# Gated recurrence of the second block as one block triangle of scores, ahead of the memory heads

## The chip, the cores and the metric

The kernel runs on one core of one Trainium2 chip. The metric is the device time of the whole kernel in microseconds (us); the times given are medians over runs. The engines are TensorE (PE, with its weight loads PEld), VectorE (DVE), ScalarE (ACT), GpSimd (POOL), and SyncE (SP), which issues the weight stream.

## What is computed

The reference is a network of two blocks over 256 tokens of width 1024, all in float32. The second block has two layers. Layer 0 mixes with a gated linear recurrence (4 heads, keys of 96, values of 192, chunks of 64 tokens) and, beside it, with 4 heads of attention over a memory of 256 rows. Its core is this:

```python
def _gla(q, k, v, log_a):
    ...
    q_c = chunks(q) * (K ** -0.5)
    k_c, v_c, g_c = chunks(k), chunks(v), chunks(log_a)
    b = jnp.cumsum(g_c, axis=3)
    b_last = b[:, :, :, -1:, :]
    q_t = q_c * jnp.exp(b)
    k_t = k_c * jnp.exp(-b)
    k_end = k_c * jnp.exp(b_last - b)
    attn = jnp.where(causal, jnp.einsum('nbhck,nbhsk->nbhcs', q_t, k_t), 0.0)
    o_intra = jnp.einsum('nbhcs,nbhsv->nbhcv', attn, v_c)

    def step(state, inp):
        qt, ke, vc, dec = inp
        o = jnp.einsum('bhck,bhkv->bhcv', qt, state)
        state = dec[..., None] * state + jnp.einsum('bhck,bhcv->bhkv', ke, vc)
        return state, o
    ...
# second_block, layer 0
o = _gla(q, k, v, log_a)
o = o * lax.rsqrt(jnp.mean(jnp.square(o), axis=-1, keepdims=True) + HEAD_NORM_EPS)
mix = jax.nn.silu(r) * (o * a_norm_g)
mo = _mem_attn(qm, mkv[:, :, 0], mkv[:, :, 1])
y = jnp.concatenate([mix, mo], axis=-1) @ w_out
x = _layer_norm(DN_ALPHA * x + y, ln_mix_g, ln_mix_b)
```

The first block (attention, a bidirectional recurrence, a convolution, an MLP), the second layer of the second block (dilated attention) and the lookup stages behind both layers are the same before and after.

## The kernel before

All weights stream as panels of 1 MB through four slots. SP loads a panel into RAW when VectorE has freed the slot (`lo_ready`); ScalarE makes the high part (`hi`, L441, fp32r), VectorE the remainder (`lo`, L889), and TensorE multiplies in three products for each tile (`three`, L1460 to L1462: high by high, high by low, low by high). `hi_to(n)` and `lo_to(n)` in the programs of ScalarE and VectorE advance these two splits up to panel n; every engine's program is written out by hand in order, so where such a call stands decides what waits behind it. A panel's result stands in one of four banks PS, and `mixing_panel(u)` of ScalarE copies it out; `evicted` waits for that copy.

Layer 0 of the second block has 11 input panels (u = 0 to 10): 0 to 3 give the queries and keys GQ, GK, 4 the memory queries QM, 5 to 7 the values GV, 8 to 10 the gate rows GR. `half` runs a panel as 48 matmuls of 256 columns; in mode "rr" these are two token tiles of 24. Then come 4 output panels (`wide`, 24 matmuls of 512 columns each), whose inputs are XH and XL, the high and low part of the mixed rows, and then one panel of memory keys and values (`mem_panel(3)`).

After panel 3 TensorE makes the gate projection (L1749). ScalarE and VectorE form from it the log gates, their scan B, the three decay factors, and at L1162 to L1164 KE (keys to the end of the chunk), KTD (keys times the inverse decay) and QTD (queries times the decay). TensorE meanwhile runs panels 4 and 5. The memory heads follow (`attention_pe`, `attention_act`, `attention_dve`): scores of heads 0 and 1 (L1524), panel 6, and for each head turn (four transposes of the probabilities, L1537), the scores of the head after next, a panel, and values (L1547). The softmax runs on VectorE (maximum L861, scaled maximum L862, reciprocal L868, scaling L870) and ScalarE (exponentials L419, copies L406 and L410), with one `lo` behind each head on VectorE.

Only then comes the recurrence: transposes of KE (L1773), scores within the four chunks (L1779), mask (L1181, L1183, with the constant "causal"), products of keys and values for three chunks (L1787), the state STA updated on VectorE (L1191, L1193), and for chunk 0 to 3 the outputs: scores times values (L1801) plus queries times state (L1803), each chunk behind the state and the copy GO of the one before. ScalarE copies each chunk (L677) and squares it (L681), after having formed the sigmoid of all gates at once (L671, L465, L466). VectorE multiplies the gates and the norm in (L1197, L1199, L1202). 11 warm matmuls (L1445), 12 transposes (L1812), the splits to XH (L686) and XL (L1245), 7 warm matmuls, and the output panels begin. GpSimd reloads the turned memory rows into MEMH and MEML (L1423) when `gon_ready` tells that the gated rows are done, as these two share storage with GV, GR and GO.

Of the kernel before, what the change touches and what calls it, by code (L numbers as in the profile page):

```python
# [6 lines left out]
F32 = mybir.dt.float32  # L7
# [4 lines left out]
ALU = mybir.AluOpType  # L12
# [3 lines left out]
P = 128  # L16
# [82 lines left out]
for _n, _w in (("ident", 128), ("iota", 128), ("zero", 128), ("blk", 128), ("ones", 128), ("rot", 128),  # L99
               ("cos", 256), ("sin", 256), ("gscan", 64), ("causal", 64)):  # L100
    CONST[_n] = (_c, _c + _w)
    _c += _w
# [28 lines left out]
def build(nc, stream, x_in, mem_in, const_in, par_in, lb_in, par2_in, wg2_in, mask_in, lev_in, rows_in, sk_in, out):  # L131
    ctx = ExitStack()
    with ctx:
# [115 lines left out]
        KER = at("ker", [P, TT, 4 * GLA_K])  # L249
        ATT = at("att", [P, 8, GLA_C])  # L250
        STA = at("sta", [P, 4, GLA_V])
# [69 lines left out]
        UC = [[M[0], M[1]], [PS[0], PS[1]]]  # L321
# [110 lines left out]
        def _(act):  # L432
# [165 lines left out]
            for l in range(DEPTH):  # L598
# [19 lines left out]
                def mixing_panel(u):  # L618
# [15 lines left out]
                if l == 0:  # L634
# [16 lines left out]
                    mixing_panel(5)  # L651
                else:
                    mixing_panel(0)

                p0 = 6 if l == 0 else 1
                attention_act(act, a, 16 + 4 * l, MEM_H, HEAD ** -0.5, lambda n: MIX2[64 * (n % 2):64 * (n % 2) + 64, 6 + n // 2, :],
                              lambda n: 64 * (n % 2), PM2, PT2,
                              panel=lambda n: mixing_panel(p0 + n))
                p1 = p0 + MEM_H + 1
# [4 lines left out]
                if l == 0:  # L664
                    mix_high(6, 8)
                    hi_to(s0 + N_MIX2[l] + 3)
                    act.wait_ge(sem("ket_done"), 1)
                    for tt in range(TT):
                        ins = act.activation(KER[:, tt, :], M[2 + tt][:, 0:384], ACT.Copy)
                    a.step(ins, sem("ker_ready"))  # L670
                    a.step(act.activation(flat(RG[:]), flat(GR[:]), ACT.Exp, scale=-1.0))  # L671
                    sigmoid(flat(RG[:]), sem("rsig_ready"))
                    for ch in range(4):
                        rows = slice(64 * (ch % 2), 64 * (ch % 2) + 64)
                        act.wait_ge(sem("oc_done"), ch + 1)
                        for j in range(2):
                            ins = act.activation(GO[rows, ch // 2, 384 * j:384 * j + 384], M[2 + j][rows, 0:384], ACT.Copy)  # L677
# [1458 lines left out]
```

## Time and profile before

| what | value |
| --- | --- |
| median of 3 runs | 2829.1 us (2828.31 to 2829.38) |
| the profiled execution | 2834.74 us |
| its span | 2832.8 us |
| mean granted TensorE clock | 0.985 |
| PE busy | 2751.9 us |
| DVE busy | 1703.8 us |
| ACT busy | 1373.9 us |
| DMA | 516.02 MB, mean 182 GB/s |

The profile is of one execution. Times inside it count from the first instruction. A granted clock of 1.00 is 2.4 GHz, of 0.50 is 1.2 GHz. A float32 matmul that is not split into high and low parts shows as two records, so "x4" is two such matmuls. A busy engine is not the same as an engine that holds up the end: the chain of waits follows from the last instruction back to whatever released each step.

### The profile page before, as it was taken

The page shows a single profiled execution, that of the slowest core. Times are in us where ns is not written, and L with a number is a line of the kernel's source. Part 1 is how long each engine was busy: PE and PEld are TensorE (multiplying, and loading weights), DVE is VectorE, ACT ScalarE, POOL GpSimd, SP SyncE. Part 2 cuts the span into 40 slices and gives each one's busy share as a digit, 9 for nine tenths or more (in the row PEclk, how much of TensorE's full clock was granted, in tenths as well). Part 3 has the DMA queues.
Part 4 walks back from the last instruction along what each step waited for, and adds up shares of the span by engine and source line. Part 5 has one row for each costly group of instructions (what it writes and reads, how often), then busy time and mean ns, then how long its engine had stood idle before and what let it go on. Part 6 is the DMA issues. An engine that isn't in the chain of part 4 may idle for free.

```text
span 2832.8 us, 45743 instructions
## 1 busy us (share of the span) xinstructions
PE 2751.9 (97%) x18622; PEld 2490.2 (88%) x18622; DVE 1703.8 (60%) x2676; ACT 1373.9 (49%) x1727; POOL 135.6 (5%) x68
## 2 busy tenths in 40 slices
PE   8989999899999999999999999998999999999997
PEld 8869889699786999999999888987999999999886
DVE  5637546465453699945554566557799654555665
ACT  4445443554344358844444444344568644444443
POOL 0000000000000430000000000000600000000000
PEclk9999999999997999999999999999999999999999
DMA  5315552145542435666656566423446756565672
GB/s 212 105 60 199 191 212 90 60 167 193 186 149 79 160 139 201 233 252 222 207 208 216 210 240 252 180 92 135 150 141 247 282 194 222 194 220 201 231 265 89
DMA packets 74411, 516.02 MB, mean 182 GB/s; under 512 B 8273, under 2 KB 8545, under 8 KB 18593
## 3 DMA queue, kind: packets, MB, share of 16 engines
q1 hardware_dynamic: 58576, 424.70, 42.1%
q0 software_dynamic: 10208, 43.45, 4.5%
q10 hardware_dynamic: 5488, 45.94, 3.9%
q8 instruction: 97, 1.59, 0.2%
q14 instruction: 42, 0.34, 0.0%
HBM read 474.22 MB, written 39.85 MB: 181 GB/s over the span
## 4 chain that ended last, share of the span: by engine, by line
PE 88%; DVE 9%; ACT 1%; issue 1%; DMA 1%; ACTq 0%; DVEq 0%
PE lin L1460 17%; PE lin L1461 17%; PE lin L1462 17%; PE m L1461 8%; PE m L1460 8%; PE m L1462 8%; PE m L1921 4%; PE lin L1633 2%; DVE lo L889 1%; PE m L1577 1%; PE m L1445 1%; PE m L1598 1%; PE m L1801 0%; PE m L1900 0%; PE m L1821 0%
## 5 line engine op out<-in xcount | busy, mean ns | idle before, releaser
L889 DVE TENSOR_TENSOR lo<-raw,hi 128x2048 fp32r<-128x2048 f32 x357 | 816.1, 2291 | 680.7 <-ACT hi L441 679.6
L441 ACT ACTIVATE hi<-raw 128x2048 fp32r<-128x2048 f32 x403 | 768.8, 1910 | 488.4 <-PE m L1462 346.8
L1460 PE MATMUL lin<-xh,hi 128*128 128x256 f32 x3376 | 975.6, 289 | 13.4 <-DVE lo L889 5.6
L1461 PE MATMUL lin<-xl,hi 128*128 128x256 f32 x3376 | 957.1, 284 | 0.0
L1462 PE MATMUL lin<-xh,lo 128*128 128x256 f32 x3376 | 956.8, 283 | 0.0
L1460 PEld LDWEIGHTS lin<-xh,hi 128*128 128x128 f32 x3376 | 647.2, 192 | 22.5 <-DVE lo L889 6.8
L1461 PEld LDWEIGHTS lin<-xl,hi 128*128 128x128 f32 x3376 | 648.0, 192 | 3.7 <-issue 1.0
L1462 PEld LDWEIGHTS lin<-xh,lo 128*128 128x128 f32 x3376 | 647.4, 192 | 0.0
L1461 PE MATMUL m<-lo,ah 128*128 128x512 f32 x1024 | 402.9, 393 | 0.0
L1460 PE MATMUL m<-hi,ah 128*128 128x512 f32 x1024 | 400.7, 391 | 0.0
L1462 PE MATMUL m<-hi,al 128*128 128x512 f32 x1024 | 399.0, 390 | 0.0
L754 ACT ACTIVATE h<-lin 128x512 f32<-128x512 f32 x128 | 76.2, 596 | 353.6 <-PE lin L1462 330.2
L1460 PEld LDWEIGHTS m<-hi,ah 128*128 128x128 f32 x1024 | 192.4, 188 | 42.3 <-DVE al L1353 0.7
L1462 PEld LDWEIGHTS m<-hi,al 128*128 128x128 f32 x1024 | 192.3, 188 | 41.8
L1461 PEld LDWEIGHTS m<-lo,ah 128*128 128x128 f32 x1024 | 192.4, 188 | 37.3
L1921 PE MATMUL m<-ob,oa 128*128 128x128 f32 x1024 | 135.2, 275 | 0.0
L1921 PEld LDWEIGHTS m<-ob,oa 128*128 128x128 f32 x1024 | 125.3, 191 | 0.5
L1430 POOL TENSOR_TENSOR lo<-raw,hi 128x2048 fp32r<-128x2048 f32 x22 | 101.4, 4608 | 336.4 <-DVE lo L889 288.0
L1460 PE MATMUL lin<-hi,xh 128*128 128x256 f32 (+2 forms) x336 | 111.7, 332 | 3.8 <-DVE xl L904 2.3
L1461 PE MATMUL lin<-lo,xh 128*128 128x256 f32 (+2 forms) x336 | 109.6, 326 | 0.0
L1462 PE MATMUL lin<-hi,xl 128*128 128x256 f32 (+2 forms) x336 | 109.4, 326 | 0.0
L1337 DVE TENSOR_SCALAR ob<-cst,pb,pf 128x128 f32<-128x128 f32 x384 | 109.4, 342 | 0.0
(332 smaller groups left out, 2856.4 us busy)
## 6 DMA issues: line engine op xcount, KB each, us to landing
raw<-stream SPq DMA_DIRECT2D x403, 1024.0 KB, 4.8
gate_table<-stg ACTq DMA_DIRECT2D x16, 2048.0 KB, 10.7
g<-gate_table POOLq DMA_DIRECT2D x32, 1024.0 KB, 8.3
rows<-rows ACTq DMA_DIRECT2D x4, 1024.0 KB, 7.5
memh<-mem_turned_scratch POOLq DMA_DIRECT2D x3, 1024.0 KB, 5.5
meml<-mem_turned_scratch POOLq DMA_DIRECT2D x3, 1024.0 KB, 9.4
x_scratch<-x ACTq DMA_DIRECT2D x2, 1024.0 KB, 4.3
x<-x_scratch ACTq DMA_DIRECT2D x2, 1024.0 KB, 7.2
```

The source lines that it names most:

```text
L441: act.activation(HI[i % SLOTS][:], RAW[:, i % SLOTS, :], ACT.Copy).then_inc(hi_ready, 1)
L754: act.activation(H[:, s % AHEAD, :], PS[s % 4][:], ACT.Gelu).then_inc(sem("ge_ready"), 1)
L889: dve.tensor_tensor(LO[i % SLOTS][:], RAW[:, i % SLOTS, :], HI[i % SLOTS][:].bitcast(F32), ALU.subtract).then_inc(lo_ready, 1)
L1337: ins = dve.tensor_scalar(ob[:, j, :], cst("iota"), PB[:, 1, t + j:t + j + 1], PF[:, t + j:t + j + 1], ALU.is_equal, ALU.mult)
L1430: pool.tensor_tensor(LO[i % SLOTS][:], RAW[:, i % SLOTS, :], HI[i % SLOTS][:].bitcast(F32), ALU.subtract).then_inc(lo_ready, 1)
L1445: pe.matmul(bank[:, 0:256], cst("ident"), CST[:, 0:256], start=True, stop=True)
L1460: pe.matmul(out_, ah, bh, start=first, stop=False, **kw)
L1461: pe.matmul(out_, ah, bl, start=False, stop=False, **kw)
L1462: return pe.matmul(out_, al, bh, start=False, stop=last, **kw)
L1577: last[j] = pe.matmul(to[:, 64 * tt:64 * tt + 64].rearrange("p (b m) -> p b m", m=m), KS[o, d, t], halves(QS[o, d, t], m)[:, :, 1 - d, :], ...
L1633: pe.matmul(PS[1][:, 256 * ct:256 * ct + 256], DG[:, n % DIAGS, :], UP[:, ct, i:i + TOK], start=(i == 0), stop=(i == CONV_K - 1))\
L1921: ins = pe.matmul(M[k % 4][:, KEYS * t:KEYS * t + KEYS], oa[:, t, :], ob[:, t, :], start=True, stop=True)
```

## The change

The chunk states go. For each head the scores of all four chunks of queries against all chunks of keys at or before them are formed at once, as a block triangle: within a chunk from KTD and QTD, against the chunk before from KE and QTD, and against earlier ones from KE and queries that VectorE has multiplied by the decays of the chunks between (QA, QB, from the columns BL). AT0 holds the scores of the first 128 keys against 256 queries, AT1 those of the last 128 keys against the last 128 queries. The diagonal blocks of 128 are masked by GM, a full 128x128 causal mask that VectorE forms from "iota" and a column of P2 in place of the constant "causal"; the part of AT0 without mask is copied by ScalarE. The outputs are then 12 matmuls of 192 columns with AT0 and AT1 as weights.

The order: scores stand behind panel 6, panel 7 after them, then the value products, and the memory heads move into panels 8, 9 and 10. `half` calls `between(0)` between its two token tiles in mode "rr", and the memory heads' scores, turns and values stand there and between the panels. ScalarE and VectorE have this order written out instead of calling `attention_act` and `attention_dve`. On ScalarE each gate panel also goes through an exponential into RG when it is evicted, and `gate(j)` forms the sigmoid of that panel; the squares are 8 of 128 rows. VectorE multiplies each gate panel (`gated_rows`), and multiplies norm and gate into GO2 by head and token tile in 8 instructions, each pair of which raises `gon_ready`. The transposes begin at its second raise, the XH and XL splits go by pairs, the memory part is split between pairs 2 and 3, and the output panels wait for the first four rows of XH and XL, the last two for all. Warm matmuls are 9 and 4 in place of 11 and 7. GpSimd's reload waits for the fourth `gon_ready`.

The core of the diff:

```diff
+                        if u >= 8:
+                            ins = act.activation(RG[:, :, 256 * j:256 * j + 256], b[:].rearrange("p (t n) -> p t n", t=2), ACT.Exp, scale=-1.0)
...
+                    mixing_panel(6)
+                    for j in range(2):
+                        act.wait_ge(sem("gmask_ready"), j + 2)
+                        a.mark(act.activation(AT0[:, 2 * j:2 * j + 2, P:TOK], M[j][:].rearrange("p (h q) -> p h q", h=2)[:, :, P:TOK], ACT.Copy), sem("gcross_ready"))
+                    mixing_panel(7)
+                    for j, bank in enumerate((3, 0, 1, 2)):
+                        tt, c = j // 2, 2 * GLA_V * (j % 2)
+                        act.wait_ge(sem("gval_done"), j + 1)
+                        a.mark(act.activation(GO[:, tt, c:c + 2 * GLA_V], M[bank][:, 0:2 * GLA_V], ACT.Copy), sem("go_ready"))
...
+                    squares(0)
+                    exps(0)
+                    squares(1)
+                    exps(1)
+                    rstd(SMALL[:, 48:56], SMALL[:, 48:56], GLA_V, EPS, sem("grs_ready"))
+                    mixing_panel(8)
+                    turned(0)
+                    exps(2)
+                    gate(0)
+                    head_out(0)
+                    turned(1)
+                    exps(3)
+                    mixing_panel(9)
+                    head_out(1)
+                    gate(1)
+                    turned(2)
+                    mixing_panel(10)
+                    gate(2)
+                    head_out(2)
+                    turned(3)
+                    head_out(3)
...
+                    v.mark(later(QA[k96, :, 0:GLA_C], QTD[k96, :, 2 * GLA_C:3 * GLA_C], 1))
+                    v.step(later(QB[k96], QTD[k96, :, 3 * GLA_C:4 * GLA_C], 2))
+                    v.step(later(QA[k96, :, GLA_C:2 * GLA_C], QB[k96], 1), sem("glater_ready"))
+                    lo_to(s0 + 9)
...
+                        v.step(dve.scalar_tensor_tensor(out=out_, in0=cm, scalar=3.0e38, in1=bank.rearrange("p (h q) -> p h q", h=heads)[:, :, 0:P],
+                                                        op0=ALU.mult, op1=ALU.min))
+                        v.mark(dve.scalar_tensor_tensor(out=out_, in0=cm, scalar=-3.0e38, in1=out_, op0=ALU.mult, op1=ALU.max), sem("gmask_ready"))
+                    masked(AT1[:], M[2][:], 4, 1)
+                    masked(AT0[:, 0:2, 0:P], M[0][:], 2, 2)
+                    masked(AT0[:, 2:4, 0:P], M[1][:], 2, 3)
...
+                    head_max(0)
+                    head_max(1)
+                    lo_to(s0 + 10)
+                    head_scale(0)
+                    head_max(2)
+                    lo_to(s0 + 11)
+                    head_scale(1)
+                    head_max(3)
+                    gated_rows(0)
+                    head_scale(2)
+                    lo_to(s0 + N_MIX2[l] + 1)
+                    gated_rows(1)
+                    head_scale(3)
+                    gated_rows(2)
+                    dve.wait_ge(sem("dve_step"), v.count["dve_step"])
+                    dve.wait_ge(sem("grs_ready"), 1)
+                    dve.wait_ge(sem("go_ready"), 4)
+                    for h in range(4):
+                        c = slice(GLA_V * h, GLA_V * h + GLA_V)
+                        for tt in range(TT):
+                            ins = dve.scalar_tensor_tensor(out=GO2[:, tt, c], in0=GO[:, tt, c], scalar=SMALL[:, 48 + 4 * tt + h:49 + 4 * tt + h], in1=RG[:, tt, c],
+                                                           op0=ALU.mult, op1=ALU.mult)
+                        v.mark(ins, sem("gon_ready"))
...
+                    pe.wait_ge(sem("gqk_ready"), 1)
+                    def chunk(n):
+                        return slice(GLA_C * n, GLA_C * n + GLA_C)
+                    keys = slice(0, 64), slice(64, 128)
+                    def two_chunks(to, h, n):
+                        pe.matmul(to[keys[0], 0:GLA_C], KTD[k96, h, chunk(n)], QTD[k96, h, chunk(n)], start=True, stop=True)
+                        pe.matmul(to[keys[1], 0:P], KTD[k96, h, chunk(n + 1)], QTD[k96, h, GLA_C * n:GLA_C * n + P], start=True, stop=True)
+                        return pe.matmul(to[keys[0], GLA_C:P], KE[k96, h, chunk(n)], QTD[k96, h, chunk(n + 1)], start=True, stop=True)
+                    for h in range(4):
+                        ins = two_chunks(M[2][:, P * h:P * h + P], h, 2)
+                    ins.then_inc(sem("gsc_done"), 1)
+                    for j in range(2):
+                        for h in (2 * j, 2 * j + 1):
+                            to = M[j][:, 256 * (h % 2):256 * (h % 2) + 256]
+                            two_chunks(to, h, 0)
+                            pe.matmul(to[keys[1], P:P + GLA_C], KE[k96, h, chunk(1)], QTD[k96, h, chunk(2)], start=True, stop=True)
+                            pe.wait_ge(sem("glater_ready"), 1)
+                            pe.matmul(to[keys[0], P:TOK], KE[k96, h, chunk(0)], QA[k96, h, :], start=True, stop=True)
+                            ins = pe.matmul(to[keys[1], P + GLA_C:TOK], KE[k96, h, chunk(1)], QB[k96, h, :], start=True, stop=True)
+                        ins.then_inc(sem("gsc_done"), 1)
+                    mixing_panel(7)
+                    for u in (5, 6, 7):
+                        evicted(pe, s0 + u)
+                    def head_values(bank, tt, h0):
+                        for h in (h0, h0 + 1):
+                            to, c = M[bank][:, GLA_V * (h - h0):GLA_V * (h - h0) + GLA_V], slice(GLA_V * h, GLA_V * h + GLA_V)
+                            ins = pe.matmul(to, AT0[:, h, P * tt:P * tt + P], GV[:, 0, c], start=True, stop=(tt == 0))
+                            if tt == 1:
+                                ins = pe.matmul(to, AT1[:, h, :], GV[:, 1, c], start=False, stop=True)
+                        ins.then_inc(sem("gval_done"), 1)
+                    pe.wait_ge(sem("gmask_ready"), 2)
+                    head_values(3, 0, 0)
+                    pe.wait_ge(sem("gmask_ready"), 3)
+                    pe.wait_ge(sem("gcross_ready"), 2)
+                    head_values(0, 0, 2)
+                    head_values(1, 1, 0)
+                    head_values(2, 1, 2)
...
+                    evicted(pe, s0 + 4)
+                    def first_scores(c):
+                        if c == 0:
+                            pe.wait_ge(sem("go_ready"), 2)
+                            scores(0)
+                            pe.wait_ge(sem("go_ready"), 3)
+                            scores(1)
+                    def second(c):
+                        if c == 0:
+                            values(0)
+                            turn(1)
+                            scores(3)
+                    def third(c):
+                        if c == 0:
+                            turn(2)
+                    mixing_panel(8, first_scores)
+                    pe.wait_ge(sem("go_ready"), 4)
+                    turn(0)
+                    scores(2)
+                    mixing_panel(9, second)
+                    values(1)
+                    mixing_panel(10, third)
+                    values(2)
+                    turn(3)
+                    warm(9, PS[(s0 + N_MIX2[l]) % 4])
+                    values(3)
+                    for kt in range(6):
+                        if kt % 2 == 0:
+                            pe.wait_ge(sem("gon_ready"), (2, 3, 4)[kt // 2])
+                        if kt == 4:
+                            pe.wait_ge(sem("pt_ready"), 16 + MEM_H)
+                        for tt in range(TT):
+                            c = 256 * (kt % 2) + P * tt
+                            ins = pe.transpose(M[kt // 2][:, c:c + P], GO2[:, tt, P * kt:P * kt + P], cst("ident"))
+                        if kt % 2 == 1:
+                            ins.then_inc(sem("got_done"), 1)
...
+                        if u == 0:
+                            warm(4, PS[(s0 + N_MIX2[l] + 3) % 4])
+                        pe.wait_ge(sem("mix2l_ready"), u // 2 + 1)
```

Removed are the transposes of KE, KER, ATT, STA, the key and value products L1787, the per chunk outputs L1801 and L1803, the whole-array gate and norm products, and the wait of the recurrence for all panels and all memory heads.

## Rows read from the trace of the kernel before

**Rows 1.** The page, parts 1 and 4: busy time, and the chain by engine.

```profile
PE 2751.9 (97%) x18622; PEld 2490.2 (88%) x18622; DVE 1703.8 (60%) x2676; ACT 1373.9 (49%) x1727; POOL 135.6 (5%) x68
...
PE 88%; DVE 9%; ACT 1%; issue 1%; DMA 1%; ACTq 0%; DVEq 0%
```

**Rows 2.** Windows: busy us of PE, PEld, DVE, ACT, POOL; granted clock; DMA.

```profile
840.00:860.00 20.00, 19.56 (x149) 17.46 (x147) 5.34 (x5) 8.63 (x14) 0.00 (x0) 1.00 0.29 106
860.00:911.00 51.00, 46.27 (x181) 27.75 (x182) 18.28 (x27) 21.16 (x55) 1.06 (x2) 0.63 0.16 62
```

**Rows 3.** Chain of waits, recurrence and output panel: start, us, engine, tile, line.

```profile
860.03 0.88 PE m L1773 x8
...
895.96 7.21 PE m L1445 x22
...
908.08 0.50 PE lin L1460
```

**Rows 4.** Timeline of TensorE, 813 to 828: start, us, line, shapes, idle before.

```profile
813.96 1.14 PE L1524 MATMUL m<-kvl,qm 64*128 64x256 f32 x8
815.03 0.39 PE L1460 MATMUL lin<-hi,xh 128*128 128x256 f32 x1
...
820.77 0.28 PE L1462 MATMUL lin<-hi,xl 128*128 128x256 f32 x1
824.55 0.66 PE L1537 MATMUL m<-cst,pm 128*128 128x128 f32 x4 [3.50 <-DVE pm L870]
...
826.90 0.58 PE L1460 MATMUL lin<-hi,xh 128*128 128x256 f32 x1
```

**Rows 5.** Timeline of TensorE, 858 to 909.

```profile
860.84 1.15 PE L1779 MATMUL m<-qtd,ktd 96*64 96x64 f32 x32
...
904.32 3.19 PE L1445 MATMUL m<-cst 128*128 128x256 f32 x14
```

**Rows 6.** Timeline of VectorE, 815 to 909.

```profile
818.18 1.21 DVE L1164 SCALAR_TENSOR_TENSOR qtd<-gq,exa 96x1024 f32<-96x1024 f32 x1
819.43 2.29 DVE L889 TENSOR_TENSOR lo<-raw,hi 128x2048 fp32r<-128x2048 f32 x1
821.64 0.69 DVE L861 TENSOR_REDUCE small<-m 128x2 f32<-128x512 f32 x1
...
823.88 0.61 DVE L870 TENSOR_SCALAR pm<-pm,small 128x256 f32<-128x256 f32 x2
...
862.04 0.69 DVE L1181 SCALAR_TENSOR_TENSOR att<-cst,m 128x512 f32<-128x512 f32 x1 [0.67 <-PE m L1779]
...
878.38 1.39 DVE L1193 SCALAR_TENSOR_TENSOR sta<-sta,bl,lin 96x192 f32<-96x192 f32 x4 [10.75 <-PE m L1803]
...
905.46 2.44 DVE L1245 SCALAR_TENSOR_TENSOR xl<-m,p,xh 128x256 fp32r<-128x256 f32 x6 [1.94 <-ACT xh L686]
```

**Rows 7.** Timeline of ScalarE, 858 to 865.

```profile
858.59 0.60 ACT L626 ACTIVATE gr<-lin 128x512 f32<-128x512 f32 x1 [3.36 <-PE lin L1462]
...
861.85 1.48 ACT L671 ACTIVATE rg<-gr 128x1536 f32<-128x1536 f32 x1
```

**Rows 8.** Chain of waits between panels 7 and 8.

```profile
835.26 1.01 PE m L1547 x4
...
837.91 0.32 PE lin L1460
```

**Rows 9.** Windows at and after falls of the clock.

```profile
159.80:163.20 3.40, 1.93 (x9) 1.38 (x10) 1.42 (x6) 0.67 (x2) 0.00 (x0) 1.00 0.01 2
163.30:166.60 3.30, 3.30 (x9) 1.40 (x8) 1.44 (x5) 1.02 (x4) 0.00 (x0) 0.50 0.00 0
...
825.00:827.00 2.00, 2.00 (x7) 1.06 (x5) 1.52 (x1) 2.00 (x7) 0.00 (x0) 0.61 0.51 213
832.00:836.00 4.00, 4.00 (x30) 3.52 (x29) 0.00 (x0) 0.60 (x1) 0.00 (x0) 0.97 0.84 281
```

**Rows 10.** Timeline of GpSimd: the reload of the turned memory rows.

```profile
901.49 0.53 POOL L1423 DMA_DIRECT2D memh<-mem_turned_scratch  x1 [341.86 <-DVE go L1202]
```

More of the change, by code:

```diff
@@ L1165, in _, with later @@
                                                     op0=ALU.mult, op1=ALU.mult), sem("gqk_ready"))
-                p0 = s0 + (6 if l == 0 else 1)
-                lo_to(p0 + 3)
-                attention_dve(dve, v, 16 + 4 * l, MEM_H, HEAD ** -0.5, PM2, between=lambda n: lo_to(p0 + 4 + n))
+                    def later(out_, in_, ch):
+                        decay = BL[k96].rearrange("p (h n) -> p h n", n=4)[:, :, ch].unsqueeze(2).to_broadcast([GLA_K, 4, GLA_C])
+                        return dve.tensor_tensor(out_, in_, decay, ALU.mult)
@@ L1481, in half @@
                     for tt in range(TT):
+                        if tt == 1:
+                            between(0)
                         for k in range(KT):
@@ L1738, in _, with mixing_panel @@
                         half(HP_SHARED + u, "cc" if u < 3 else "rr", inst=6 if u == 0 else None)
-                def mixing_panel(u):
-                    half(s0 + u, "rr" if l == 0 and u >= 5 else "cc", inst=4 if l == 0 and u == 0 else None)
+                def mixing_panel(u, between=lambda c: None):
+                    half(s0 + u, "rr" if l == 0 and u >= 5 else "cc", inst=4 if l == 0 and u == 0 else None, between=between)
                 if l == 0:
@@ new lines, in _, with scores @@
+                    pe.wait_ge(sem("gmask_ready"), 2)
[5 more added lines that the diff above has]
+                    head_values(2, 1, 2)
+                    def scores(n):
+                        if n >= 2:
+                            pe.wait_ge(sem("exp_ready"), 16 + n - 1)
+                        o = slice(64 * (n % 2), 64 * (n % 2) + 64)
+                        for qt in range(2):
+                            ins = pe.matmul(M[n % 2][:, 256 * qt:256 * qt + 256], QM[o, n // 2, P * qt:P * qt + P], KVL[o, 256 * (n // 2):256 * (n // 2) + 256],
+                                            start=True, stop=True)
+                        ins.then_inc(sem("sc_done"), 1)
@@ new lines, in turn @@
+                    def turn(n):
+                        pe.wait_ge(sem("sm_ready"), 16 + n + 1)
+                        if n >= 1:
+                            pe.wait_ge(sem("pt_ready"), 16 + n)
+                        for kt in range(2):
+                            for qt in range(2):
+                                ins = pe.transpose(M[2][:, 256 * kt + P * qt:256 * kt + P * qt + P], PM2[:, n % 2, qt, P * kt:P * kt + P], cst("ident"))
+                        ins.then_inc(sem("pt_done"), 1)
@@ new lines, in values @@
+                    def values(n):
+                        pe.wait_ge(sem("pt_ready"), 16 + n + 1)
+                        if n >= 1:
+                            pe.wait_ge(sem("o_ready"), 16 + n)
+                        o = 64 * (n % 2)
+                        for kt in range(2):
+                            c = 512 + 256 * kt + 64 * n
+                            ins = pe.matmul(M[3][o:o + 64, 0:256], KVL[:, c:c + 64], PT2[:, n % 2, kt, :], start=(kt == 0), stop=(kt == 1))
+                        ins.then_inc(sem("pv_done"), 1)
```

208 lines of the change are left out of this document (87 added, 121 removed).

## Prediction

> **What bounds the kernel now.** I read the page first: TensorE is busy 97% of the span and carries 88% of the chain that ended last [rows 1]. What pays is therefore time taken off TensorE's own program, or time in which it waits or runs at the lower of its two clock levels. Then the windows: between the input panels it is at full level, and around the recurrence it averages 0.63 over 51 us [rows 2]. The chain of waits shows why: between the last input panel and the first output panel every link is the recurrence, with products L1773 and L1779, chunk states L1787, outputs L1801 and L1803 chunk after chunk behind the state update on VectorE, 22 records of warm matmuls, transposes, and the split into XH and XL [rows 3]. TensorE's timeline gives the ends of the stretch that I sum: panel 5 ends when the scores of heads 0 and 1 begin at 813.96, and the chain has the first output panel at 908.08 [rows 3, 4]. That is 94.1 us from 813.9. Everything behind 908.08 is moved as a whole.
>
> **What is removed.** From 860.03 to 908.08 lie 48.05 us that hold only the recurrence, its gates and the split [rows 3]. No weight panel runs there, and the clock was at 1.2 GHz for most of it: the 22 records of warm matmuls took 7.21 us [rows 2, 3]. The wait of 3.50 us for the first head's softmax goes too [rows 4], in its old form.
>
> **What stands in its place, in TensorE's order.** The work is 5 panels (6 to 10) and small pieces. I start at 813.9.
> - Panel 6: 48 matmuls, first start 815.03, last start 820.77 [rows 4], so 5.76 us with the last step; end 819.65. VectorE's qtd ends at 818.18 + 1.21 = 819.4 [rows 6]; the new wait for it costs about nothing. The mask tile GM is formed on VectorE ahead of the gate projection, in a wait of VectorE; nothing late depends on it.
> - Score stage: 4 heads of 256 columns, then 4 of 512, 3072 columns in 64-column tiles. L1779 did 1024 such columns (32 records, 16 matmuls) in 1.15 us [rows 5], with the two halves of the array alternating as here. So 3.4 us. Bounds: 2.7 us if the halves overlap fully, 5.5 us if not at all (3072 columns at 1.78 ns: 14 records, 7 matmuls of 256 columns on the full array, took 3.19 us [rows 5]). I take 3.4, the same tile form. QA, QB and QA again are 256 elements each on VectorE, at 0.41 as in L1245 [rows 6], ready at 820.7 while TensorE is still in the first four heads.
> - Panel 7: 5.76. Then TensorE waits for its eviction (0.60 on ScalarE [rows 7]): 0.7. This is a new wait; queued behind it are the value products and panel 8. The masks are long done: behind the weight split at 820.7 (2.29) VectorE needs 1.4 for the first and 0.8 for each of the others (0.69 for 512 elements [rows 6]), 826.1 in all, against panel 7's end at 828.8.
> - Value products: 12 matmuls of 192 columns on the full array, 0.34 us each by the same 1.78 ns, 0.38 by the two accumulating ones of 256 columns in 1.01 [rows 5, 8]: 4.2 us. They replace 28 matmuls of the same 192 columns on quarter and three-quarter tiles.
> - Panel 8 with scores 0 and 1 in its middle: 5.76 + 1.16 [rows 4]. It ends at 840.4.
> - A wait for the first softmax. From the scores at 836.3: matmuls 1.1, maximum 0.69 + 0.2 with its scaling, the second maximum 0.9, the weight split 2.29 that stands ahead of head_scale, then 0.17 + 0.61 and steps [rows 6]: 842.4. So 2.0 us idle, where the kernel before had 3.5.
> - turn(0) and scores(2): 1.65; panel 9: 5.76; in its middle values(0), turn(1), scores(3): 2.65, the distance from 835.26 to 837.91 [rows 8], and 0.2 of waiting, as one more split stands ahead of head_scale(1); values(1) 1.0; panel 10: 5.76, with turn(2) 0.6 in it. It ends at 860.2.
> - The tail. On TensorE: values(2), turn(3), 9 warm matmuls of 0.46 [rows 5], values(3), half of the transposes: about 7.4. Longer is the gate: evict 0.6, exponential 0.5, logarithm and exponential 0.63 each (512 elements; the whole array took 1.48 for 1536 [rows 7]), product 0.69, 8 products of 192 elements at 0.35 (L1193: 1.39 for 4), weight split 2.29, four XL pieces at 0.41 [rows 6]: 10.1. First output panel at 870.3.
>
> Sum: 5 x 5.76 = 28.8; 3.4 + 0.7 + 4.2 + 1.16 + 2.0 + 1.65 + 2.65 + 0.2 + 1.0 + 0.6 = 17.6; tail 10.1; together 56.5 against 94.1. Gain 37.6 us at full clock.
>
> **The clock.** In the kernel before, 3.5 us of idleness ahead of 824.55 put TensorE at the lower level, 1.2 GHz, just behind it [rows 9]. It cost: panel 7 took 835.26 - 826.90 = 8.36 instead of 5.76, and the turn and scores ahead of it 826.90 - 824.55 = 2.35 instead of 837.91 - 836.27 = 1.64 (836.27 is where values end): 3.3 us [rows 4, 8]. In the first block a stretch with 1.93 us busy of 3.40, all in small pieces, was at full level, and the one behind it at 0.50 [rows 9]. The new wait of 2.0 us lies between two small pieces, so I expect one fall there. It costs what one fall costs, 3.3, and nothing hides it, because from there to panel 10's end TensorE sets the pace and the tail hangs on panel 10. Net gain 34.3.
>
> **What else moves.** ScalarE gets an exponential more for each gate panel and 8 squares of 128 rows for 16 of 64 rows; up to panel 10 they lie beside panels, and hide as long as turned(n) is done before values(n): 846.1 against 846.9 for head 0. That 0.8 us is the thinnest cover; if it goes, TensorE waits by the excess. Splits of panels 9 and 10 on VectorE start 14 us later than before, so SP issues weights 13 and 14 later, at 841.5 and 847.2; with some 5 us to land they are there before ScalarE asks at 857.7 and later. On GpSimd the reload of the turned memory hangs on gon_ready, at 901.49 before [rows 10], now near 866, still 26 us ahead of its panel. The stage from the first output panel on has the same program; its own waits (the keys of the next product among them) may meet the clock differently, by which I allow half of one fall, 1.7 us, either way. The weight split of panel 12 now stands between the normed rows and XL: it is in the tail above.
>
> **A rule weighed.** In the trace a change of tile form costs a longer first matmul: 0.39 behind the scores at 815.03, where the later ones show 0.28 [rows 4]. The Trainium skill (TensorEngine Tiling (Array Packing), Key Properties) says that changing the tiling mode drains TensorE, while different tiles of one mode run in parallel. By the first half each inserted piece costs its own drain, which the distances above already hold; by the second half the score stage would come to its lower bound of 2.7, and the gain to 0.7 more.
>
> **Rivals.**
> - *No fall of the clock.* The clock stays at 2.4 GHz through the 2.0 us of waiting. For it: with 19.56 of 20 us busy from 840 to 860 the short waits between panels left it there [rows 2]; the one fall in this stretch had 3.5 us. Gain 37.6: 2791.5 us.
> - *Two falls or thin cover.* The score stage of 3.4 us, all on 64-column tiles, brings a fall of its own (3.3), or its halves do not overlap (+2.1), or values(0) waits. For it: the clock was down for most of the stretch of 64-row and 64-column tiles from 860 on [rows 2, 3]. Against: the scores at 813.96, on 64 rows, did no harm [rows 4]. 2829.1 - 34.3 + 3.3 = 2798.1, with the missing overlap 2800.2.
> - *Slower than before.* TensorE falls to 1.2 GHz in the score stage and does not come back until the four output panels are through. Then the 45 us of its work in the stretch (37.7 up to panel 10's end, 7.4 behind it) takes twice as long, which eats the gain and 2 us more, and the output panels (4 of as many columns as an input panel, so 23 us) take twice as long as well: 2829.1 + 2 + 23 = 2854. It decides from 75 us of TensorE's work at the lower level on. Against it: after the fall near 825 a single panel was enough for the clock to return: 0.97 from 832 to 836 [rows 9].
> - *It does not do what it says.* A wait left out of my list (a bank, a count of a semaphore) holds panels back so that the recurrence stays exposed by half: gain about 20, 2809.
>
> **How the numbers follow.** The profiled execution took 2834.7 us (span 2832.8, 1.9 around it), 5.6 above the median 2829.1; the same differences apply to both: after, 2800.4 profiled and 2829.1 - 34.3 = 2794.8 as the median. Chances: forecast (one fall) 0.50; no fall 0.25; two falls or thin cover 0.17; half exposed 0.06; slower 0.02. Range: the ends are no fall with the score stage at its lower bound and the later stage 1.7 better (2791.5 - 0.7 - 1.7 = 2789.1), and two falls with the missing overlap and 1.7 worse (2801.9). A measurement of this kernel can tell about 0.2%, 5.7 us. All cases but the last lie far beyond it: faster 0.97, same 0.01, slower 0.02.
>
> **What the changed profile would show.** The output panels start about 870 (873.5 with the fall) and not 908; the 51 us window at 0.63 is gone; there is one idle spell of 2 us ahead of turn(0), and behind it a stretch at 1.2 GHz; the score stage takes 3.4 us; panel 10 ends near 860 to 863.5; L889 and XL end the tail on VectorE, not the warm matmuls. I am wrong if TensorE idles over 1 us at any other place of 814 to 860, or if the tail is longer than 10 us.

## The result

The changed kernel takes 2795.97 us as the median of 4 executions (2793.34 to 2797.59), where the kernel before beside it took 2829.24: 33.3 us less, a ratio of 0.9877 (95% interval 0.9864 to 0.9889). Forecast were 2794.8 us in a range of 2789.1 to 2801.9. The profiled execution took 2793.34 us.

The page of the changed kernel, parts 1 and 4, answers [rows 1]:

```profile
span 2791.1 us, 45655 instructions
...
PE 2716.9 (97%) x18588; PEld 2472.1 (89%) x18588; DVE 1701.7 (61%) x2680; ACT 1369.1 (49%) x1713; POOL 135.7 (5%) x68
...
PE 89%; DVE 9%; ACT 1%; issue 1%; DMA 1%; ACTq 0%; DVEq 0%
```

TensorE is as full as before, 97%; its busy time is 35 us less, and part of that is work that no longer runs at 1.2 GHz. Windows of the new stretch (busy us of PE, PEld, DVE, ACT, POOL; granted clock; DMA) answer [rows 2]:

```profile
820.00:838.00 18.00, 17.11 (x161) 16.32 (x158) 6.04 (x10) 7.23 (x18) 0.00 (x0) 1.00 0.17 59
838.00:850.00 12.00, 9.98 (x65) 7.94 (x65) 7.94 (x14) 10.07 (x30) 0.00 (x0) 1.00 0.41 140
896.00:912.00 16.00, 13.64 (x96) 12.73 (x96) 10.62 (x13) 4.88 (x8) 3.71 (x1) 1.00 0.60 210
```

In these windows, and in all others that I read between 820 and 970, the clock is at 2.4 GHz in this execution. What TensorE still waited for between 780 and 910 (total, times, longest):

```profile
PE lin L1552 <- DMA sk<-keys: 2.4, 1, 2.4
PE m L1911 <- DVE pm L1249: 2.0, 1, 2.0
PE m L1883 <- ACT gv L627: 0.9, 1, 0.9
```

These are the two waits that the forecast names in the stretch (eviction of panel 7, scaling of head 0), and the wait for the keys behind it. The chain of waits, in order of time, shows the pieces and the tail, and answers [rows 3, 8]:

```profile
818.80 0.20 PE m L1859
...
827.67 0.60 ACT gv L627
...
828.53 1.86 PE m L1883 x10
...
838.48 2.29 DVE lo L936
840.88 0.63 DVE pm L1249 x2
...
841.64 0.63 PE m L1911 x4
...
859.63 0.60 ACT gr L627
...
860.75 0.64 ACT rg L466
...
862.14 0.70 DVE rg L1256
862.87 2.73 DVE go L1278 x8
865.60 2.20 DVE lo L936
867.80 1.58 DVE xl L1331 x4
869.42 0.50 PE lin L1552
```

L1859 begins the scores, L1883 the value products, L936 (lo) is the weight split that stands ahead of head 0's scaling (pm), and from 859.63 on the chain runs through ScalarE and VectorE to the first output panel at 869.42. The warm matmuls are not on it, as forecast.

### The profile page after: what moved, and what is told of

Read it like the earlier page. It is cut to its first block, busy times and chain, and to the rows that moved or that the text cites. A ratio compares the mean times of both kernels' runs of the same rounds, so it can differ in the third digit from the quotient of the medians.

```text
span 2791.1 us, 45655 instructions
## 1 busy us (share of the span) xinstructions
PE 2716.9 (97%) x18588; PEld 2472.1 (89%) x18588; DVE 1701.7 (61%) x2680; ACT 1369.1 (49%) x1713; POOL 135.7 (5%) x68
## 4 chain that ended last, share of the span: by engine, by line
PE 89%; DVE 9%; ACT 1%; issue 1%; DMA 1%; ACTq 0%; DVEq 0%
PE lin L1552 17%; PE lin L1554 17%; PE lin L1553 17%; PE m L1553 8%; PE m L1554 8%; PE m L1552 8%; PE m L2082 4%; PE lin L1727 2%; DVE lo L936 1%; PE m L1671 1%; PE m L1692 1%; PE m L2061 0%; PE m L1981 0%; PE m L1800 0%; PE m L1704 0%
## 5 line engine op out<-in xcount | busy, mean ns | idle before, releaser
L936 DVE TENSOR_TENSOR lo<-raw,hi 128x2048 fp32r<-128x2048 f32 x357 | 816.0, 2291 | 673.7 <-ACT hi L442 672.6
```

What stands on the lines that cost most here:

```text
L936: dve.tensor_tensor(LO[i % SLOTS][:], RAW[:, i % SLOTS, :], HI[i % SLOTS][:].bitcast(F32), ALU.subtract).then_inc(lo_ready, 1)
```

## The steps against the rows

I measure the stretch from the start of the gate projection, which both kernels have, to the first output panel. The projection starts here, before and after:

```profile
800.36 1.96 PE L1749 MATMUL m<-gq,wg 16*96 16x256 f32 x8
799.37 1.96 PE L1843 MATMUL m<-gq,wg 16*96 16x256 f32 x8
```

The stretch is 800.36 to 908.08 before and 799.37 to 869.42 after. That is 107.7 against 70.05 us, 37.7 less; the sum said 37.6 at full clock. Its terms:

| term | forecast, us | profile after, us |
| --- | --- | --- |
| scores, L1859 to panel 7's start (818.73 to 821.62) | 3.4 | 2.9 |
| panel 7 and its eviction (821.62 to 828.53; 0.9 of it is the wait) | 6.5 | 6.9 |
| value products (828.53 to 832.37) | 4.2 | 3.8 |
| panel 8 with scores(0) and (1) (832.37 to 839.66) | 6.9 | 7.3 |
| wait for head 0's scaling | 2.0 | 1.98 |
| turn(0) and scores(2) (841.64 to 843.26) | 1.65 | 1.6 |
| panel 9 with its pieces, and values(1) (843.26 to 853.15) | 9.6 | 9.9 |
| panel 10 with turn(2) (853.15 to 859.52) | 6.4 | 6.4 |
| tail, from values(2) to the output panel (859.52 to 869.42) | 10.1 | 9.9 |

The sum comes out so closely because its misses cancel: scores, value products and tail are together 1.1 us shorter than forecast, panels 7 to 9 with what hangs on them 1.1 us longer. The fall of the clock behind the 1.98 us wait, 3.3 us in the forecast, is not in this execution. That, and the difference between an execution and the median, is what the first experiments are for.

## Experiments

The intervals of single kernels against the kernel before are some 0.15%, or 4 us, wide to either side. So kernels are compared by their stretch in the trace first and by their times second.

**1. How the executions spread.** The changed kernel unaltered.

> The changed kernel unaltered, to see how its executions spread (2793.3 and 2794.4, 2797.6 and 2797.6 so far) and which falls of TensorE's clock another profiled execution has. Theory A (a fall of the clock decides): the times stand in two groups about 3.4 us apart, near 2793.5 and 2797, and the mean granted clock goes with them, about 0.994 and 0.992. Theory B (something else, such as transfers, spreads the times): the clock is the same in both groups.

2795.08 us median (2794.62 to 2796.93, ratio 0.9878, 0.9861 to 0.9894). The times stand closer than in two groups; the profiled execution, 2794.66 us at a clock of 0.992, has other falls than the first one (2793.34 at 0.994). Windows of it:

```profile
838.00:850.00 12.00, 11.34 (x65) 9.58 (x66) 6.60 (x14) 8.63 (x22) 0.00 (x0) 0.86 0.49 177
896.00:912.00 16.00, 13.63 (x85) 12.80 (x84) 9.04 (x10) 4.47 (x6) 4.58 (x1) 0.89 0.53 202
```

Here the clock does fall behind the wait ahead of the first turn (0.86 in 838 to 850) and again at the wait for the keys (0.89 in 896 to 912); both stood at 1.00 in the first profile. The stretch is 71.4 us long (796.39 to 867.80) instead of 70.05: the fall cost 1.4 us, not 3.3. The loss lies in the first half of panel 9, 843.26 to 846.32 in the first profile and 840.27 to 844.83 here. So the mechanism of the forecast is there, in one execution and not in the other, and its price was taken from a fall that cost more. For the spread of the whole time this decides little by itself: within a clock given in thousandths (0.001 of the span is 2.8 us) theory B is not excluded. Experiment 4 comes back to it.

**2. The wait taken away.** On VectorE:

```diff
+                    lo_to(s0 + 10)
                     head_max(0)
                     head_max(1)
-                    lo_to(s0 + 10)
                     head_scale(0)
```

> On VectorE the weight split of panel 9 stands ahead of the first two maxima, where VectorE was idle for 11.8 us, and no longer between them and the scaling of head 0. TensorE's wait ahead of the first turn (1.98 us in the changed kernel) goes. Theory A1 (the random fall sits at this wait): 2.0 us less and no second group: 2791.4, all within 1 us. Theory A2 (the random fall sits at the wait for the keys of the next product, 2.36 us): 2.0 less in both groups, 2791.5 and 2795. If the split is late for panel 9 instead: no gain.

2792.98 us median (2789.93 to 2796.05; ratio 0.9872, 0.9854 to 0.989). The wait is gone, and another stands in its place:

```profile
PE m L1883 <- ACT gv L627: 0.9, 1, 0.9
PE m L1921 <- ACT pt L683: 0.8, 1, 0.8
```

The stretch is 68.9 us (795.69 to 864.60), 1.1 less than in the changed kernel: 1.98 gained, 0.8 given back, as values(0) now comes before ScalarE's copy of head 0's turned probabilities. This is the cover of 0.8 us that the forecast called the thinnest. The four executions still fall into 2790 and 2796, two of each, so A1 is wrong: most of the spread does not come from this wait. The window of the keys had 0.89 here too.

**3. The wait made longer.**

```diff
                     head_max(0)
                     head_max(1)
-                    lo_to(s0 + 10)
+                    lo_to(s0 + 11)
                     head_scale(0)
```

> The wait ahead of the first turn made longer: the splits of panels 9 and 10 both stand ahead of the scaling of head 0, so TensorE waits 4.2 us there instead of 2.0. If a fall of the clock follows a long enough wait: 2793.4 + 2.2 + 3.3 = 2799 in every execution, and the profile shows 1.2 GHz behind the wait. If only the wait itself counts: 2795.6 and 2799 in two groups as before.

2799.03 us median (2796.2 to 2801.78; ratio 0.9893, 0.9876 to 0.9909). Wait and windows:

```profile
PE m L1911 <- DVE pm L1249: 4.2, 1, 4.2
...
838.00:850.00 12.00, 10.43 (x43) 8.40 (x44) 3.03 (x9) 6.05 (x12) 0.00 (x0) 0.60 0.41 166
```

The wait is 4.2 us, and the clock is at 0.60 over the 12 us around and behind it. The stretch is 75.7 us (795.10 to 870.84), 5.7 more than in the changed kernel: 2.2 of wait and 3.5 of clock. So in the one execution profiled a wait of 4.2 us has the full price of the kernel before, and a wait of 2 us costs part of it and not in every execution. That the long one costs it in every execution, as expected, is not shown: the four times fall into two groups again, 2796.2 and 2796.9 against 2801.2 and 2801.8, and the profiled one is among the shorter.

**4. The wait for the keys filled.** Six warm matmuls ahead of `keys_loaded`.

> Six warm matmuls ahead of the wait for the keys in both layers, so TensorE is busy during that wait (2.36 us in layer 0). If the random fall sits there (A2): the second group vanishes, all near 2793.5, or 1 us above if six are too many. If it sits at the wait ahead of the first turn (A1): two groups as before.

2796.46 us median (2792.69 to 2797.99; ratio 0.988, 0.9863 to 0.9897). The spread is not smaller, so A2 falls as well: neither of the two waits alone makes it. The traces show a larger source in the first block, which no kernel here changes. The window from 536 to 555 has a clock of 0.82 in the first profile and 0.55 in that of experiment 1. An earlier one, in the first profile and in that of experiment 1:

```profile
156.00:192.00 36.00, 30.90 (x125) 20.58 (x125) 12.98 (x31) 14.04 (x33) 0.00 (x0) 0.86 0.00 1
156.00:192.00 36.00, 31.25 (x140) 22.32 (x140) 13.86 (x31) 18.07 (x35) 1.13 (x2) 0.95 0.09 33
```

With the higher clock the same work is done earlier. VectorE's first split of the memory rows (`meml`, L1130) starts at 191.26 in the first profile and at 186.48 in that of experiment 1. The thirteen profiles of this document fall into two groups by it: 186.0 to 186.9 in five and 191.3 to 192.7 in eight, with nothing between. That is 5 us of the whole time, clock and time go together as theory A has it, and the place is neither A1's nor A2's. The profiled executions of experiments 2 and 3, each one of the two shorter of its four times, are both among the five; the longer ones were not profiled, so that they belong to the eight is likely and not shown. What decides which of the two an execution takes I have not tested.

**5. The block triangle without its new place.** The scores, masks and value products as in the changed kernel, but behind all panels and memory heads, with `attention_pe`, `attention_act` and `attention_dve` as before and the gates over the whole array.

```diff
-                    mixing_panel(6)
+                    evicted(pe, s0 + 4)
+                    attention_pe(16, MEM_H, ..., panel=lambda n: mixing_panel(6 + n))
+                    pe.wait_ge(sem("o_ready"), 16 + MEM_H)
...
-                    mixing_panel(7)
...
-                    warm(9, PS[(s0 + N_MIX2[l]) % 4])
+                    warm(12, PS[(s0 + N_MIX2[l]) % 4])
```

> The block triangle alone, in the place where the recurrence stood in the kernel before: behind all panels and memory heads, the gates formed over the whole array. Theory (both parts count, the smaller work more than the cover): from panel 10's end to the first output panel 3.4 or less for the scores, 1.5 until the masks, 4 for the values, 0.5 copy, 2 squares, 0.5, 2.8 products, transposes and splits 3.5: 18 to 24 us instead of 48; the wait ahead of the first turn with its fall is back. So 25 to 29 us less than before: 2801 to 2805. Rival (the cover brings the gain, the new form of the work little): under 15 us less, 2815 or more.

2803.87 us median (2801.32 to 2806.52; ratio 0.9907, 0.989 to 0.9923). The chain behind panel 10, and TensorE's waits:

```profile
859.72 1.02 PE m L1572 x4
861.19 0.27 PE m L1797
...
864.26 1.49 ACT rg L657
865.77 0.66 ACT at L660 x2
866.43 1.38 ACT rg L466
867.84 1.48 ACT rg L467
869.32 1.52 ACT go L665 x4
...
875.17 1.42 DVE go L1209 x4
```

```profile
PE m L1562 <- DVE pm L878: 4.7, 1, 4.7
PE m L1839 <- DVE go L1209: 1.4, 1, 1.4
```

The stretch is 79.4 us (800.59 to 879.98): 28.3 less than before, while the changed kernel has 37.7. So about three quarters of the gain are the new form of the work (no states, and 12 value products on the full array for 28 on parts of it, and no 38 us at 1.2 GHz, the half level that makes 0.63 of 51 us [rows 2]), and 9.3 us are what the new order brings. The chain also shows what is left without the cover: ScalarE's whole-array exponentials and the copies and squares. The old wait for the first softmax is back with 4.7 us, and with it a fall of the clock, 0.81 over 820 to 838: the turn and scores behind the wait and panel 7 take 3.0 us (825.97 to 829.01) and 7.4 (829.01 to 836.36), together 3.0 more than at full clock. Against the changed kernel, that is 2.7 us of wait and 3.0 of clock, so 5.7 of the 9.3 us are this wait and its fall.

**6. The gates over the whole array.** Only `gate`, `gated_rows` and the exponential at the eviction are undone.

```diff
-                        if u >= 8:
-                            ins = act.activation(RG[:, :, 256 * j:256 * j + 256], ..., ACT.Exp, scale=-1.0)
...
-                        sigmoid(RG[:, :, 256 * j:256 * j + 256], sem("rsig_ready"))
+                        if j == 2:
+                            a.step(act.activation(flat(RG[:]), flat(GR[:]), ACT.Exp, scale=-1.0))
+                            sigmoid(flat(RG[:]), sem("rsig_ready"))
```

> The changed kernel with the gates formed over the whole array behind panel 10 instead of panel by panel. The tail hangs on them: exponential 1.48, logarithm 1.48, exponential 1.48 and product 1.76 in place of 0.5, 0.63, 0.63 and 0.69: 3.7 us more, 2799. Rival (warm matmuls and values cover it): no difference, 2795.

2799.01 us median (2798.84 to 2801.07; ratio 0.9895, 0.9878 to 0.9911). Its chain of waits in the tail:

```profile
860.87 1.50 ACT rg L692
862.38 1.49 ACT rg L466
863.90 1.49 ACT rg L467
...
865.49 1.77 DVE rg L1257
867.28 2.72 DVE go L1279 x8
870.00 2.20 DVE lo L937
```

The stretch is 73.9 us (799.90 to 873.83), 3.9 more against 3.7 expected. The tail does hang on the gates; warm matmuls and values cover nothing of it. Of the 9.3 us of the new order, 3.9 are the gates panel by panel. With the 5.7 us of experiment 5 that already makes slightly more than the whole. As an estimate from these two experiments, then, moving the scores and value products themselves between the panels gained nothing that shows; TensorE sets the pace there, and they take its time in either place.

**7. The two halves of the array apart.** The 36 score matmuls in another order: for each bank all with output in the lower 64 partitions, then all in the upper.

> The same score matmuls, but for each bank all with output in the lower 64 partitions first and then all in the upper 64, so that neighbours no longer use different halves of the array. If alternating halves overlapped: the score stage grows from 2.72 us (818.73 to 821.45) to 5.1 to 5.5. If the time per matmul is set by something else (issue, weight loads): it stays near 2.7.

One execution, 2797.4 us. The first and last score matmuls and the panel behind them:

```profile
817.06 0.33 PE L1868 MATMUL m<-qtd,ktd 96*64 96x64 f32 x2
...
821.11 0.28 PE L1885 MATMUL m<-qb,ke 96*64 96x64 f32 x2
821.32 0.39 PE L1552 MATMUL lin<-hi,xh 128*128 128x256 f32 x1
```

The stage takes 4.26 us (817.06 to 821.32) where the changed kernel has 2.89, both at full clock. So neighbours on different halves do overlap, and the order inside `two_chunks` is worth 1.4 us. It did not reach 5.1: where a lower group meets an upper one, the trace shows the two running side by side still, and the columns alone would be 5.5 at the forecast's 1.78 ns. I expected more because I counted no overlap at these borders.

**8. Three repairs together.** The split of panel 9 as in experiment 2; ScalarE's copy for head 0 ahead of panel 8's eviction; the split of panel 12 ahead of the last gate product, with 7 and 3 warm matmuls.

```diff
                     exps(1)
+                    turned(0)
                     rstd(SMALL[:, 48:56], SMALL[:, 48:56], GLA_V, EPS, sem("grs_ready"))
                     mixing_panel(8)
-                    turned(0)
...
                     head_scale(3)
+                    lo_to(s0 + N_MIX2[l] + 2)
                     gated_rows(2)
...
-                    warm(9, PS[(s0 + N_MIX2[l]) % 4])
+                    warm(7, PS[(s0 + N_MIX2[l]) % 4])
```

> Three repairs together: the split of panel 9 ahead of the first maxima (alone it took away the 1.98 us wait, but a wait of 0.8 us for the copy of head 0's turned probabilities came in its place), that copy ahead of the eviction of panel 8, and the split of panel 12 ahead of the last gate product, with 7 and 3 warm matmuls in place of 9 and 4. 2.0 us from the first two, 1 us from the third: 2792 as the median, 3 less than the changed kernel. Rival: the falls of the clock elsewhere are wider than this, and 5 rounds show no difference.

2789.87 us median (2785.48 to 2791.74; ratio 0.9855, 0.9839 to 0.9872). TensorE's waits:

```profile
PE lin L1553 <- DMA sk<-keys: 2.4, 1, 2.4
PE m L1884 <- ACT gv L627: 0.9, 1, 0.9
PE lin L1553 <- DVE xl L1332: 0.5, 1, 0.5
```

The stretch is 67.1 us (800.75 to 867.87), 2.9 less than in the changed kernel's first profile. As the intervals of both kernels overlap, I measured them again side by side, with one more.

> The changed kernel unaltered once more, as the base for the two kernels beside it on the same chip: 2795 as the median, executions between 2793 and 2798.

> The three repairs once more, beside the unaltered kernel on the same chip. By the waits removed in the trace (1.98 us ahead of the first turn, 1.6 us in the tail, 0.45 of it given back) it is 3.2 us faster; with one fall of the clock less in part of the executions up to 5. If the first measurement (2789.9 against 2795) was chance of the clock's falls: medians within 2 us.

Unaltered 2794.19 us (2793.72 to 2794.81; ratio 0.9871, 0.9856 to 0.9886), repaired 2792.83 (2787.88 to 2793.54; ratio 0.986, 0.9845 to 0.9876). The second difference is 1.4 us where the first was 5, and by the expectation, which put medians within 2 us down to chance in the first measurement, it speaks for chance. The two profiled executions beside each other say why whole times do not settle it. From the gate projection to the output panel they have 71.4 and 67.1 us, 4.3 less for the repaired kernel, as only the unaltered one has the fall behind its wait; but the repaired one comes to the gate projection 4.6 us later (800.57 against 795.99), by the first block of experiment 4. Over both measurements the repaired kernel has 8 executions from 2785.5 to 2793.5 (middle 2791.7), the unaltered one 12 from 2793.3 to 2797.6 (middle 2794.6). That fits the 2.9 us of the stretch, but the two sets of times touch, and the whole times alone do not show the gain. The traces do: both profiles of the repaired kernel have a stretch of 67.1 us, and those of the unaltered one 70.05, 71.4 and 71.4.

**9. The keys first.** The repaired kernel, with the two lines on ScalarE's queue exchanged:

```diff
+                act.dma_start(SK[:], sk_in[l]).then_inc(sem("keys_loaded"), 16)
                 act.dma_start(x_scr, X[:]).then_inc(sem("x_spilled"), 16)
-                act.dma_start(SK[:], sk_in[l]).then_inc(sem("keys_loaded"), 16)
```

> The three repairs, and the load of the keys issued ahead of the spill of X in both layers, no longer behind it on ScalarE's queue. TensorE's wait for the keys (2.4 us in layer 0, and 2.6 in layer 1 before) ends earlier if the spill of 1 MB delays the keys: up to 2 us for each layer and a fall of the clock less, 2785. If the keys' own landing time (4.6 us from issue) is what lasts: no difference from the three repairs alone.

2783.98 us median (2781.94 to 2787.54; ratio 0.9839, 0.9825 to 0.9853). The keys' issue, with the KB of one and the median us to landing, in the changed kernel:

```profile
sk<-keys ACTq DMA_DIRECT2D x1, 128.0 KB, 4.1
```

and in this one, with TensorE's waits:

```profile
sk<-keys ACTq DMA_DIRECT2D x1, 128.0 KB, 2.1
...
PE m L1884 <- ACT gv L627: 0.9, 1, 0.9
PE lin L1553 <- DVE xl L1332: 0.5, 1, 0.5
PE lin L1553 <- DVE xl L948: 0.3, 1, 0.3
```

The spill of 1 MB did delay the keys: they land 2.1 us after their issue instead of 4.1, and TensorE's waits for them, 2.4 us in layer 0 and 2.6 in layer 1, are gone. All five executions are faster than every one of the changed kernel's, and its interval lies below that kernel's beside it. So it beats the kernel before and the changed kernel. Not all of the 8.9 us against the repaired kernel beside it is the exchange. In the traces it takes off 2.1 us in each layer, 4.2 in all (last section); of the 9.2 us between the two profiled executions, 3.3 lie ahead of the gate projection, which the exchange does not touch.

## Why the prediction was right, and where it was not

The time fell by the mechanism forecast, and the steps held within 0.5 us each, in part by misses that cancel: the serial recurrence between panel 10 and the output panels is gone, TensorE sets the pace up to panel 10's end, and the tail is gates, products, weight split and XL on ScalarE and VectorE. Both waits that the forecast names are there, with 0.9 and 1.98 us, and TensorE idles over 1 us nowhere else from 814 to 860.

Several steps were off.
- *The fall of the clock* was priced at 3.3 us and taken as certain in the forecast's case. Of three profiled executions of this program, one had none in the stretch and two had one (0.86 in 838 to 850); it cost 1.4 us in both (stretches of 71.4 against 70.05). The row behind the price had a wait of 3.5 us; experiment 3 shows that price (3.5) at 4.2 us. The forecast also says that the wait lies between two small pieces. It lies behind the second half of panel 8, 24 matmuls on the full array up to 839.66. The two rivals "no fall" and "one fall" are both right, in different executions, and lie closer together than I had them.
- *An execution against the median.* I took the 5.6 us between the profiled execution and the median before as fixed and carried it over: 2800.4 us profiled. It was 2793.34. Of the 7.1 us between, 3.3 are the fall that was not there. 3.1 more are behind the stretch, up to the first product with the keys (51.8 us before, 48.7 after): the kernel before had its clock at 0.72 in 940 to 952, at and behind its wait for the keys, the changed kernel 1.00 in 896 to 912, where it waits for them. 1.0 more lies ahead of the gate projection, in work that both have alike. The executions of the kernel before near 2830 us have a clock of 0.985 to 0.987, those near 2835 of 0.985; that the slower ones have more falls fits this, but three digits do not resolve it. So the profiled times differ by 41.4 us, the medians by 33.3, and the stretch by 37.7. That the forecast met the median within 1.2 us is thus partly luck: the price of the fall that I added stands in part for differences of the clock elsewhere, which I had not reckoned. More executions move the measured gain as well: beside the kernel before it was 33.3, 35.1 and 36.2 us in the three measurements. With a fall of 1.4 us the stretch gives 36.3.
- *Scores and value products* were mis-sized, 3.4 and 4.2 for 2.9 and 3.8. The halves overlap nearly fully (lower bound 2.7), so the row of L1779 was taken at the wrong figure: its 1.15 us hold the last matmul's run to its end, while its 32 starts lie within 0.93 us (860.84 to 861.77), and three times that and a step is 2.9. 0.35 us for a product of 192 columns was 0.03 too much. The Trainium skill (TensorEngine Tiling (Array Packing), Key Properties) says that different tiles can run matmuls in parallel. The trace agrees: 2.89 us with the halves alternating and 4.26 with them apart.
- *The longer first matmul* of a panel was read as the cost of a change of tile form. But the panel behind the value products, which use the full array as it does, begins with 0.41 us (832.37) too, so the rows do not show that the change of form is what costs.
- *Small slips.* By its own terms the forecast has the first memory scores at 836.6 and the end of panel 8 at 840.6, where it says 836.3 and 840.4; it puts the tail at 10.1 us and calls itself wrong if the tail is over 10 (it was 9.9); and in the rival "slower" the 75 us are TensorE's time at the lower level, not work counted at full clock, of which 37.6 us would do. None of these moves the sum by more than 0.2 us.

Of the rivals, "two falls or thin cover" was half there: the cover of 0.8 us for values(0) held in the changed kernel and gave way as soon as experiment 2 brought TensorE forward. "Slower" and "half exposed" have nothing for them in any trace.

## What to carry to other kernels

A recurrence over a few chunks can be cheaper as one block triangle of scores: more columns in all, but no chain of state, copy and product between engines, and none of the low clock that went with it here; that alone was three quarters of the gain. The new order brought the rest by what other engines had to do (the first softmax and the gates), not by hiding TensorE's own work. What then stands ahead of the critical reply in the other engines' programs (here a weight split of 2.29 us ahead of a scaling of 0.6) is the next thing to move. Ask of a large transfer on the same queue whether a small one behind it is waited for.

## What the runs showed of the hardware

The same program on the same data has its clock falls at different places from one execution to the next. Six profiles here have the wait of 1.98 us ahead of the first turn. The window from 838 to 850 has a granted clock of 1.00 in three of them (the first profile and those of experiments 4 and 6) and of 0.86 in the other three (both repeats of the changed kernel, and experiment 7). In the three with 1.00 the first split of the memory rows starts at 191.3 to 192.5 (experiment 4), in the three with 0.86 at 186.5 to 186.9. So an execution that gains 5 us early can lose 1.4 here; why the two go together is not shown.

The times of the unaltered kernel differ by 4.3 us. The profiled executions show where such differences lie. The columns give when the gate projection starts, the stretch from there to the first output panel, the time from there to the first product with the keys in layer 0, and the rest up to TensorE's last matmul, all in us:

| profile | start | stretch | to the keys | rest |
| --- | --- | --- | --- | --- |
| kernel before | 800.36 | 107.72 | 51.78 | 1858.06 |
| changed, first | 799.37 | 70.05 | 48.66 | 1858.22 |
| changed, experiment 1 | 796.39 | 71.41 | 50.13 | 1859.73 |
| changed, experiment 8 | 795.99 | 71.45 | 50.09 | 1859.73 |
| repaired, first | 800.75 | 67.12 | 48.62 | 1858.24 |
| repaired, second | 800.57 | 67.13 | 48.61 | 1859.81 |
| keys first | 797.23 | 67.12 | 46.49 | 1856.13 |

With equal falls a stretch repeats to 0.04 us; one fall moves it by 1.4 or 1.5. The start, in work that is the same in all of them, moves by 5. A single profiled time is therefore no base to subtract from: a stretch between two instructions that both kernels have told a difference to within one fall, which its windows of the clock show, and the whole time only to within some 5 us.
